# Two attention loops: the first weight chunk of the output product split whole under the value product, the second in quarters inside the loop

## The reference

```python
def moba_nsa_mixer(h, w_in, ...):            # layer 0
    mq, mk, mv, nq, kc, vc, ksl, vsl, kwn, vwn, gz = _split(hp @ w_in, EVEN_SPLITS)
    ...  # 8 heads of block attention; 8 heads with a compressed, a selected and a window branch,
    ...  # each softmax(q k^T * scale + bias) @ v, the branches weighed by sigmoid(gz)
    return o.astype(h.dtype) @ w_out
def fox_mixer(h, w_in, b_forget, w_out):     # layer 1
    ...  # 16 heads, softmax(q k^T * scale + decay bias, causal) @ v
    return o.astype(h.dtype) @ w_out
...
h = h + mixer(...)                           # then a squared-relu MLP
```

## Time and profile before

| | |
|---|---|
| median of 3 runs | 1245.8 us (1245.62 to 1246.9) |
| profiled execution, its own time | 1246.66 us |
| its span, first to last instruction | 1244.9 us |
| PE busy | 1199.5 us (96%) |
| DVE busy | 826.1 us (66%) |
| ACT busy | 658.6 us (53%) |
| mean granted TensorE clock | 0.992 |

### The profile page before, as it was taken

One profiled execution on the slowest core, in us unless ns is written; L12 is line 12 of the kernel. 1 busy time (PEld: TensorE's weight loads), 2 busy tenths in 40 slices (PEclk: granted clock), 3 DMA queues, 4 the chain that ended last, 5 costly groups with the idle time before them and its releaser, 6 DMA issues.

```text
span 1244.9 us, 19225 instructions
## 1 busy us (share of the span) xinstructions
PE 1199.5 (96%) x7770; PEld 1050.1 (84%) x7770; DVE 826.1 (66%) x1273; ACT 658.6 (53%) x1080; POOL 237.5 (19%) x300
## 2 busy tenths in 40 slices
PE   6898999999999999999999999999999899999996
PEld 5786788888888678888888888999997698888996
DVE  5966776566576587666557876457965757767643
ACT  6427666643333666664446555435646755655532
POOL 4104521110000341211112222000003611121101
PEclk9999999999999999999999999999999899999998
DMA  7790244555453435455553554562461122555451
GB/s 279 256 234 30 76 186 184 188 218 181 159 198 133 175 117 190 173 201 183 190 203 141 198 200 140 202 237 102 152 223 69 35 88 93 193 185 187 149 201 57
DMA packets 33800, 205.56 MB, mean 165 GB/s; under 512 B 3744, under 2 KB 6320, under 8 KB 12720
## 3 DMA queue, kind: packets, MB, share of 16 engines
q1 hardware_dynamic: 30416, 200.47, 44.7%
q10 hardware_dynamic: 3296, 3.87, 1.5%
HBM read 202.87 MB, written 1.46 MB: 164 GB/s over the span
## 4 chain that ended last, share of the span: by engine, by line
PE 80%; DVE 13%; ACT 5%; issue 1%; DMA 1%; POOL 0%; POOLq 0%; ACTq 0%; DVEq 0%
PE ps L669 37%; PE ps L674 24%; PE ps L672 5%; PE ps L673 5%; DVE wl L611 3%; PE ps L693 1%; PE ps L695 1%; PE ps L694 1%; DVE tf L2226 1%; ACT wh L582 1%; DVE y L1947 1%; DVE xb L747 1%; ACT pb L924 1%; PE ps L2509 1%; DMA h<-xt 1%
## 5 line engine op out<-in xcount | busy, mean ns | idle before, releaser
L611 DVE TENSOR_TENSOR wl<-raw,wh 128x2048 fp32r<-128x2048 f32 (+3 forms) x192 | 415.7, 2170 | 141.3 <-ACT wh L582 141.3
L669 PE MATMUL ps<-xb,wh 128*128 128x512 f32 x1424 | 502.6, 398 | 4.2 <-DVE wl L611 3.7
L674 PE MATMUL ps<-xb,wl 128*128 128x256 f32 x1696 | 476.2, 281 | 0.0
L582 ACT ACTIVATE wh<-raw 128x2048 fp32r<-128x2048 f32 (+3 forms) x194 | 348.2, 1798 | 148.3 <-PE ps L674 114.6
L669 PEld LDWEIGHTS ps<-xb,wh 128*128 128x128 f32 x1424 | 267.4, 188 | 71.0 <-issue 5.4
L674 PEld LDWEIGHTS ps<-xb,wl 128*128 128x128 f32 x1696 | 321.6, 190 | 0.0
L674 PE MATMUL ps<-ab,wl 128*128 128x256 f32 x1088 | 306.6, 282 | 0.0
L669 PE MATMUL ps<-ab,wh 128*128 128x512 f32 x640 | 227.1, 399 | 0.2
L674 PEld LDWEIGHTS ps<-ab,wl 128*128 128x128 f32 x1088 | 206.4, 190 | 0.0
L669 PEld LDWEIGHTS ps<-ab,wh 128*128 128x128 f32 x640 | 120.2, 188 | 30.5 <-DVE ab L982 0.8
L866 DVE TENSOR_TENSOR tf<-ps,tf 128x256 f32<-128x256 f32 x148 | 61.8, 420 | 119.7 <-ACT tf L861 119.7
(11 more groups left out here) (324 smaller groups left out, 1343.5 us busy)
## 6 DMA issues: line engine op xcount, KB each, us to landing
raw<-wstream SPq DMA_DIRECT2D x162, 1024.0 KB, 4.8
raw<-wstream SPq DMA_DIRECT2D x32, 704.0 KB, 4.0
e_bt<-scratch ACTq DMA_DIRECT2D x16, 128.0 KB, 8.2
o_bt<-scratch SPq DMA_DIRECT2D x2, 1024.0 KB, 9.9
raw<-wstream SPq DMA_DIRECT2D x2, 560.0 KB, 8.9
raw<-wstream SPq DMA_DIRECT2D x4, 256.0 KB, 6.7
h<-xt ACTq DMA_DIRECT2D x4, 256.0 KB, 7.9
raw<-wstream SPq DMA_DIRECT2D x2, 512.0 KB, 9.8
```

Of the source, the lines that this page charges most:

```text
L582: e.g.activation(WH[i % HLN][:, 0:w], RAW[i % RAWN][:, 0:w], ACT.Copy).then_inc(S["hi"], 1)
L611: e.g.tensor_tensor(WL[q][:, 0:w], RAW[i % RAWN][:, 0:w], f32(WH[q][:, 0:w]), ALU.subtract).then_inc(S["lo"], 1)
L669: e.g.matmul(PS[b][:, :].rearrange("p (a t) -> p a t", a=2), wh[:, sl], x2[:, :, cs], start=start, stop=k == p.nk - 1, skip_group_check=pair)
L674: ins = e.g.matmul(o, wl[:, sl], xh[:, cs], start=False, stop=k == p.nk - 1, skip_group_check=pair)
```

## The change

In both attentions the first chunk of the output product (E0, O0) is no longer split in quarters. ACT splits it whole ahead of the eviction of the second value product (`ahead=1`). DVE splits it whole after the maxima of head 3 in the first attention, and ahead of the loop in the second. The second chunk (E1, O1) stays in quarters. Its high quarters now stand at i = 9, 11, 13, 15 (first) and 1, 3, 5, 7 (second), its low quarters at 16 to 19 (as before) and at 8 to 11.

```diff
 # act_even
-                    act_gemm(e, G["ev1"], drain=act_toks(G["ev1"], e_v, 512, 0), ahead=0)
+                    act_gemm(e, G["ev1"], drain=act_toks(G["ev1"], e_v, 512, 0), ahead=1)
...
-                if 6 <= i < 10 or 12 <= i < 16:
-                    hi_part(e, G["eo"].first + i // 12, i % 6)
+                if 9 <= i < 17 and i % 2:
+                    hi_part(e, G["eo"].first + 1, (i - 9) // 2)
 # dve_even
-                if 10 <= i < 14 or 16 <= i < 20:
-                    lo_part(e, G["eo"].first + i // 16, (i - 10) % 6)
+                if 16 <= i < 20:
+                    lo_part(e, G["eo"].first + 1, i - 16)
...
+                if i == 3:
+                    lo_to(e, G["eo"].first)
 # act_odd
-            act_gemm(e, G["ov1"], drain=act_toks(G["ov1"], o_v, 512, 2), ahead=0)
+            act_gemm(e, G["ov1"], drain=act_toks(G["ov1"], o_v, 512, 2), ahead=1)
...
-                if 2 <= i < 10:
-                    hi_part(e, G["oo"].first + (i - 2) // 4, (i - 2) % 4)
+                if 1 <= i < 9 and i % 2:
+                    hi_part(e, G["oo"].first + 1, i // 2)
 # dve_odd
-            dve_gemm(e, G["ov1"], 0, ahead=0)
+            dve_gemm(e, G["ov1"], 0, ahead=1)
...
-                if 6 <= i < 14:
-                    lo_part(e, G["oo"].first + (i - 6) // 4, (i - 6) % 4)
+                if 8 <= i < 12:
+                    lo_part(e, G["oo"].first + 1, i - 8)
```

## The result

The changed kernel took 1239.8 us in the median of 6 runs (1233.6 to 1244.4), the kernel before 1246.2 us beside it (6 runs, 1241.6 to 1247.5): ratio 0.9953, 95% interval 0.9931 to 0.9976. The profiled execution of the changed kernel took 1237.19 us, with a span of 1235.4; that is 9.5 us under the profiled execution of before (1246.66 and 1244.9), where the sum said 3.25.

A forecast was written before the change was run, and what follows sets the result against it. PE was busy 96% of the span, so only its waits, through DVE's low quarters (first attention) and ACT's high quarters (second), could be won: 1.95 + 1.30 = 3.25 us, median 1245.8 to 1242.6 us, range 1240.8 to 1245.0.

The forecast's parts named there:

- the sum: Both attention loops' gains added, 1.95 + 1.30 = 3.25 us, taking the median from 1245.8 to 1242.6 us.
- First loop, 1.95 forecast: First attention: removed low quarters give DVE a lead of 1.45 us, one ACT step 0.52 more; 1.95 us won.
- Cost of both: nothing.: Whole splits of E0 and O0 hide before the loops, sparing 3.4 and 2.5 us, then 4.1 and 3.0.
- Second loop, 1.30 forecast: Second attention: ACT loses four of eight quarters, then PE's work and DVE's low quarters bind; 1.30 us won.
- Behind about 132.7 and 437.6 us PE no longer waits: Late in both loops `pe_begun` fills PE, so a lead that PE has there stays.
- One sign that I had named as fatal: Second loop: the forecast is wrong if PE still waits for ACT at the turns after i = 7.
- The other two signs: The forecast is wrong if the evictions move from about 102.3 and 416.9, or first-loop lead does not pass 1.45.
- A rule against the trace.: DVE/POOL exclusion rule: two low quarters overlapping POOL take 0.99 and 0.91 us, others 0.67 and 0.66; removal frees 2.91.
- the rival sum: Low quarters taken without contention (4 x 0.58): first loop gains 0.59 us less, time 1243.2 us.
- the walk: Step-by-step tracing of waits through both loops, winning 1.95 and 1.30 us; gain over 2.5 us given chance 0.60.
- The slower rival: Second attention: O0 lands too late, delaying ACT's eviction; landing at 419.6 would make 1248.3 us; chance 0.04.
- Lead lost between engines: Rival for both loops: DVE's lead is partly lost at other engines' waits, gain 0.8 to 2.4 us, 1244.2; chance 0.28.

The follow-up runs named there:

- E0: Not a run: the first chunk of the output product in the first attention, which the changed kernel splits whole instead of in quarters.
- even only: The change made in the first attention alone, against the kernel before: ratio 0.9958, again 0.9972; first-attention loop stretch 30.88 and 30.86 us, second-attention 22.99 and 22.98.
- high parts only: Changed kernel, but low parts of E0 and O0 stay in quarters on DVE at the old places: loop stretches 32.39 (first attention) and 21.81 us (second).
- after again: The changed kernel, unchanged, run a third time against the kernel before: 1237.2 us, ratio 0.9965; loop stretches 30.86 and 21.38 us.
- even a: A profile of the kernel with the change in the first attention alone; its first-attention loop stretch took 31.38 us.
- even b: Another profile of the kernel with the change in the first attention alone; its first-attention loop stretch took 30.88 us.

## Why the prediction was off, point by point

**The step that failed** is the last of the sum, "so the median becomes 1245.8 - 3.2 = 1242.6 us", with the range of 4.2 us around it. It takes the three runs of before, 1.3 us apart, for a fixed number, and its range holds only unknown costs of the edit. But one program varies by more than that: further sets of the kernel before had medians of 1246.2 (6 runs, those three among them), 1245.4 (12), 1244.9 (35), 1242.4 (23), 1242.1 (29) and 1241.1 (12), over several chips, and single executions from 1235.4 to 1249.4.

It was not that the base beside the result was low: it stood 0.4 us above 1245.8. With the gain of 3.6 us that the stages show, 1246.2 makes 1242.6, inside the range and by luck the forecast itself. The 2.8 us from there to the measured 1239.8 are not in the stages; the six executions of the changed kernel lay between 1233.6 and 1244.4, and such a spread can make them. In the repeats the medians differ by 5.8 and 4.9 us, also more than 3.6. As a gain, 3.25 us is a ratio of 0.9974, inside all three intervals of the changed kernel (0.9953, 0.9967, 0.9965; in the first by 0.0002), as is the 0.9971 by the stages. All three lie below both: whether the change wins something outside the stages is not shown, and not excluded.

What of the first 9.5 us is whose: 3.64 us is what the schedule wins where its cover holds (0.9 of it was lost in that one execution, below); the 3.0 and 3.7 ahead of and between the stages lie where the change does nothing, and profiles of one kernel differ by as much: 3.3 between the stages in the first two profiles of before, 2.2 in the length of the value product over all eighteen.

**First loop, 1.95 forecast, 2.03 measured** (1.1 in the first profile, next point). Right in each wait that takes the lead, shown by even only and by high parts only (0.53 for the 0.52).

**"Cost of both: nothing."** Right in two of the three profiles of the changed kernel, wrong in the first one: the spare of 3.4 and 2.5 us was read off an execution in which PE ran the first half of the value product near the lower clock level, and I took it for a property of the schedule. The stretches over the product, of before, of the run "after again" and of the first profile after:

```profile
93.70:98.50 4.80, 4.80 (x23) 4.76 (x22) 1.72 (x13) 3.24 (x16) 2.50 (x6) 0.52 0.00 0
98.50:102.30 3.80, 3.80 (x32) 3.65 (x32) 0.00 (x0) 0.02 (x1) 0.00 (x0) 1.00 0.00 0
```

```profile
93.50:97.00 3.50, 3.50 (x21) 3.46 (x20) 1.66 (x12) 3.50 (x17) 1.66 (x4) 0.70 0.00 0
97.00:100.70 3.70, 3.70 (x31) 3.69 (x29) 2.01 (x1) 1.66 (x1) 0.00 (x0) 1.00 0.00 0
```

```profile
92.80:99.00 6.20, 6.20 (x50) 6.20 (x48) 2.61 (x18) 5.12 (x18) 1.67 (x4) 1.00 0.00 0
```

Granted clock 0.52 and then 1.00, 0.70 and then 1.00, and 1.00 throughout (1.00 is 2.4 GHz, the lower level 1.2 GHz): the product took 8.21, 7.08 and 6.18 us. PE waits and does short work between the two value products, and the clock fell there or did not. The Trainium skill, page "TensorE: Matmul & The Clock Gate", section "What's actually happening", says that the point of change varies between runs of one kernel; the traces agree that it varies. In the first profile after, a late load of the bias came on top: DVE waited 0.74 us for it ahead of its first maxima, and all that follows on ACT and DVE was later. Timeline of ACT, DVE, PE:

```profile
93.21 0.29 DVE L933 CUSTOM_DVE_ANT_0 pb<-ps,e_bt 128x128 f32<-128x128 f32 x1 [0.74 <-DMA e_bt<-scratch]
...
97.43 1.91 ACT L582 ACTIVATE wh<-raw 128x2048 fp32r<-128x2048 f32 x1
99.27 0.88 ACT L872 ACTIVATE e_v<-ps,rb 128x280 f32<-128x280 f32 x2
...
99.37 2.29 DVE L611 TENSOR_TENSOR wl<-raw,wh 128x2048 fp32r<-128x2048 f32 x1 [2.87 <-ACT wh L582]
...
101.65 0.27 DVE L933 CUSTOM_DVE_ANT_0 pb<-ps,e_bt 128x128 f32<-128x128 f32 x1
...
102.72 0.55 PE L916 MATMUL ps<-consts,pb 128*128 128x128 f32 x3 [0.97 <-POOL pb L972]
```

No idle time is left between the low part and the maxima, and PE waits 0.97 us for POOL, behind DVE's reciprocal: stage 1 is 31.81 instead of 30.88. One profile of even only (the run "even a") had a product of 6.15 us, a bias load 0.29 us late, and a wait of PE for POOL of 0.55: stage 1 31.38.

Both losses shrink to the same 0.2 us when the bias wait is taken off (0.93 - 0.74 and 0.50 - 0.29). So, as an estimate, the full clock alone takes the cover past its end by 0.2 us, and the rest is the late bias. Neither alone was seen to cost 0.5: one profile (the run "even b") had a bias wait of 0.68 us with a product of 7.74 us, and its stage 1 is 30.88. Eight profiles split both parts of E0 where the changed kernel does; in the six of them with a product of 6.83 us or more, nothing was lost.

**Second loop, 1.30 forecast, 1.61 measured.** The mechanism was right: the waits for ACT's copy at turns 2, 4 and 6 are gone, and turn 1 is late. Two terms are mis-sized. PE's pair, "about 3.0 us", is 2.80: the scores were put at 1.25, near the 1.26 from their start to the end shown of their last group (425.65 to 426.91 in before), but the next group can start before that end, 1.10 after theirs (422.52 to 423.62 above). The other is the last step, below. Timeline of PE after:

```profile
414.49 0.55 PE L916 MATMUL ps<-consts,pb 128*128 128x128 f32 x3 [0.84 <-POOL pb L972]
416.10 0.52 PE L916 MATMUL ps<-consts,pb 128*128 128x128 f32 x3
...
418.92 0.50 PE L916 MATMUL ps<-consts,pb 128*128 128x128 f32 x3
...
421.72 0.50 PE L916 MATMUL ps<-consts,pb 128*128 128x128 f32 x3
...
425.17 0.52 PE L916 MATMUL ps<-consts,pb 128*128 128x128 f32 x3 [0.23 <-ACT pt L942]
...
428.48 0.52 PE L916 MATMUL ps<-consts,pb 128*128 128x128 f32 x3 [0.23 <-ACT pt L942]
```

Shifted by 416.46 - 408.64 = 7.82 to the clock of before: turn 1 422.31 (forecast 422.32), turn 2 423.92 (424.05), turn 4 426.74 (427.03), turn 6 429.54 (430.03), turn 8 432.99 (433.08), turn 10 436.30 (436.4), first piece 437.85 (438.16). The low quarters at 8 to 11 took most of what the faster pairs had won back (3.45 us from turn 6 to 8, where I had 3.05): of a lead of 0.49 over the forecast at turn 6, 0.10 is left at turn 10. The other 0.21 of the 0.31 come from the last step. "Behind about 132.7 and 437.6 us PE no longer waits" does not hold: the weight load (PEld) of the first piece waited for DVE, which had the last low quarter of O1 just ahead. Timeline of PEld before:

```profile
439.46 0.19 PEld L669 LDWEIGHTS ps<-ab,wh 128*128 128x128 f32 x1 [0.27 <-DVE nm L934]
```

In the changed kernel that quarter stands two steps earlier and the wait is gone: 0.30 us from the last turn to the first piece, where before had 0.57.

One sign that I had named as fatal did appear: PE still waits for ACT at turns 8 and 10, 0.23 each. It is not the old bound: ACT itself waits for DVE's maxima ahead of them, and DVE has the quarters, as the timeline of ACT shows:

```profile
423.67 0.40 ACT L923 ACTIVATE pb<-pb,nm 128x128 f32<-128x128 f32 x1 [1.01 <-DVE nm L934]
...
426.98 0.40 ACT L923 ACTIVATE pb<-pb,nm 128x128 f32<-128x128 f32 x1 [0.81 <-DVE nm L934]
```

The test was badly put. The other two signs, that the evictions move or that the first loop's lead does not pass 1.45, both appeared in the first profile (eviction at 99.27 instead of 102.28, lead 1.1), with the shorter product and the late bias; in the repeat they did not (102.31, lead 2.04).

**"A rule against the trace."** The rows are misread there, though the rule that it quotes fits them. All four low quarters of E0 lie beside POOL's weighing, not two. POOL's instructions beside them, each shown alone, timeline of before:

```profile
113.81 0.73 POOL L972 TENSOR_SCALAR pb<-pb,rs,e_v 128x128 f32<-128x128 f32 x1 [2.17 <-DVE rs L966]
...
115.49 0.56 POOL L972 TENSOR_SCALAR pb<-pb,rs,e_v 128x256 f32<-128x256 f32 x1
...
117.31 0.81 POOL L972 TENSOR_SCALAR pb<-pb,rs,e_v 128x128 f32<-128x128 f32 x1 [1.27 <-DVE rs L966]
...
119.62 0.56 POOL L972 TENSOR_SCALAR pb<-pb,rs,e_v 128x256 f32<-128x256 f32 x1
```

The quarters at 113.55 and 117.14 started first and took 0.67 and 0.66 us; those at 115.59 and 119.80 started behind a POOL instruction already under way and took 0.99 and 0.91. What decides is which of the two starts first. The price of the rival sum is wrong as well: by the walk, the first quarter is lost at the next wait and the copies stand at 117.10 whatever the second and third take, so without contention only 0.26 us (0.84 - 0.58) would be missing, not 0.59. No run took the contention away.

**O0 in time.** Timeline of ACT and DVE after:

```profile
403.20 1.92 ACT L582 ACTIVATE wh<-raw 128x2048 fp32r<-128x2048 f32 x1 [3.74 <-DMA raw<-wstream]
...
405.15 2.29 DVE L611 TENSOR_TENSOR wl<-raw,wh 128x2048 fp32r<-128x2048 f32 x1 [5.15 <-ACT wh L582]
...
410.25 0.29 DVE L933 CUSTOM_DVE_ANT_0 pb<-ps,o_bt 128x128 f32<-128x128 f32 x1 [2.81 <-PE ps L1750]
```

ACT waits for the landing, as forecast, and DVE is done 2.8 us before it is wanted (3.0 in the forecast). The slower rival did not occur. **Lead lost between engines** did not either: where the cover holds, both stages came out a little over the walk.

**Chances.** Faster by over 0.2% was given 0.60; all three ratios say so, but only the first interval lies wholly beyond 0.2%.

## What to carry to other kernels

Read the spare of a cover from the shortest form the cover can take: work hidden under a matmul stage that ran at the lower clock has less room when the clock stays up. Take the gain of a schedule from stages between the same instructions, and the base of a forecast from many executions; a range for a time must hold the spread of the kernel itself. For an engine's own pace, read the distance between starts in a stretch without waits, not its busy time or the ends shown. And look at the load that the first step waits for: here 0.74 us of lateness there used up a cover that the clock had already thinned.

## What the runs showed of the hardware that I had not expected

Dense matmuls run at two paces at the same granted clock, 285 against 291 in 50 us, 794 against 810 in 140 us, and the same program takes either. What chooses it was not found. The clock dip that reaches into the second value product of the first attention can be absent, short or long: the product took 6.15 to 8.36 us over eighteen profiles, with many lengths between. The paces alone put two executions of one program 9.2 us apart, and single executions differed by 12.5 us within one set (1235.4 to 1247.9), over three times what this change wins. A VectorE subtraction of 128 x 512 took 0.66 to 0.67 us where it started ahead of POOL's instruction and 0.91 to 0.99 where it started just behind one.
